# Gate tiles, a reciprocal and the first mixed input, reordered in a kernel of two transformer blocks

## What is computed

```python
# first block, in each of two layers, behind the mixers
x = x + concat(mixers) @ w_out[l]
u = rms_norm(x, mlp_norm_g[l]) @ w_up[l]
x = x + square(relu(u)) @ w_down[l]
gate = sigmoid(rms_norm(x, ple_norm_g[l]) @ w_ple_gate[l])
e = rms_norm(p[l] @ w_ple_proj[l], ple_post_norm_g[l])
x = x + gate * e                       # followed by rms_norm(x) @ next weights

# second block, second layer (RWKV-7), h = rms_norm(x, norm_tok)
xx = 0.5 * (h[t - 1] + h[t + 1]) - h   # neighbours in time, zero outside
xr = h + xx * mu[0]                    # and xw, xk, xv, xa, xg with mu[1..5]
r = xr @ w_r                           # and so on for w, k, v, a, g
```

## Time and profile before

| what | before |
|---|---|
| median of 3 runs | 3337.2 us (3335.54 to 3346.71) |
| the profiled execution | 3335.55 us, of which the profile's span is 3333.5 us |
| PE busy | 3062.7 us (92%) |
| PE weight loads busy | 2431.1 us (73%) |
| VectorE / ScalarE / GpSimd busy | 1870.9 / 1384.1 / 633.8 us |
| mean granted clock of TensorE | 0.966 of 2.4 GHz |

### The profile page before, as it was taken

How to read it: one execution, slowest core, us unless ns; L and a number is a source line. 1 busy time by engine, 2 the same in 40 slices (tenths; PEclk the granted TensorE clock), 3 DMA queues, 4 the chain that set the end, 5 groups by cost and what they waited for, 6 DMA issues and landing times. The chain is left out here.

```text
span 3333.5 us, 57339 instructions
## 1 busy us (share of the span) xinstructions
PE 3062.7 (92%) x24238; PEld 2431.1 (73%) x24238; DVE 1870.9 (56%) x2687; ACT 1384.1 (42%) x2354; POOL 633.8 (19%) x528
## 2 busy tenths in 40 slices
PE   8979999999978999999989999979788988799999
PEld 6756788887745788886757888757477777588887
DVE  6675543435675452536575746564366776457464
ACT  5545322235445421224274423335465565344232
POOL 1000220212000230302000101133164564101010
PEclk9989999999989999999899999979899999899999
DMA  4101222222101222222003322225411111033232
GB/s 154 46 1 61 86 96 97 94 92 82 64 4 45 82 95 95 95 97 76 20 1 120 100 97 95 89 101 180 152 47 38 38 45 41 18 111 103 89 101 81
DMA packets 82333, 260.91 MB, mean 78 GB/s; under 512 B 9632, under 2 KB 13216, under 8 KB 81696
## 3 DMA queue, kind: packets, MB, share of 16 engines
q1 hardware_dynamic: 71424, 235.75, 21.7%
q10 hardware_dynamic: 10656, 21.50, 1.7%
HBM read 236.25 MB, written 20.97 MB: 77 GB/s over the span
## 5 line engine op out<-in xcount | busy, mean ns | idle before, releaser
L1645 DVE TENSOR_TENSOR mlp_w_lo<-mlp_ring,mlp_w_hi 128x1024 fp32r<-128x1024 f32 (+1 forms) x211 | 251.3, 1192 | 598.3 <-ACT mlp_w_hi L1625 598.1
L1625 ACT ACTIVATE mlp_w_hi<-mlp_ring 128x1024 fp32r<-128x1024 f32 (+1 forms) x211 | 213.2, 1011 | 695.9 <-PE ps L1586 689.3
L1645 DVE TENSOR_TENSOR ffn_w_lo<-ffn_ring,ffn_w_hi 128x1024 fp32r<-128x1024 f32 (+3 forms) x172 | 222.5, 1294 | 446.9 <-ACT ffn_w_hi L1625 446.9
L1625 ACT ACTIVATE ffn_w_hi<-ffn_ring 128x1024 fp32r<-128x1024 f32 (+3 forms) x172 | 187.3, 1089 | 486.3 <-PE ps L1586 480.7
L1585 PE MATMUL ps<-mlp_more_parts,mlp_w_hi 128*128 128x512 f32 x952 | 374.6, 394 | 0.0
L1584 PE MATMUL ps<-tiles_parts,mlp_w_hi 128*128 128x512 f32 x832 | 331.0, 398 | 5.7 <-issue 5.7
L1584 PE MATMUL ps<-ffn_x_parts,ffn_w_hi 128*128 128x512 f32 x792 | 312.1, 394 | 22.7 <-DVE ffn_x_parts L2355 20.9
L1584 PE MATMUL ps<-mlp_more_parts,mlp_w_hi 128*128 128x512 f32 x760 | 307.9, 405 | 25.6 <-DVE mlp_more_parts L1698 15.0
L1586 PE MATMUL ps<-tiles_parts,mlp_w_lo 128*128 128x512 f32 x832 | 329.0, 395 | 0.0
L1585 PE MATMUL ps<-ffn_x_parts,ffn_w_hi 128*128 128x512 f32 x792 | 309.8, 391 | 0.0
L1586 PE MATMUL ps<-ffn_x_parts,ffn_w_lo 128*128 128x512 f32 x792 | 309.7, 391 | 0.0
(11 more groups left out here) (494 smaller groups left out, 6233.3 us busy)
## 6 DMA issues: line engine op xcount, KB each, us to landing
ffn_ring<-in_w_ffn_up SPq DMA_DIRECT2D x88, 512.0 KB, 3.3
mlp_ring<-in_w_up SPq DMA_DIRECT2D x64, 512.0 KB, 3.4
mlp_ring<-in_w_down SPq DMA_DIRECT2D x64, 512.0 KB, 3.4
rwkv_keep<-ffn_ring ACTq DMA_DIRECT2D x64, 256.0 KB, 2.4
sq<-rwkv_keep SPq DMA_DIRECT2D x64, 256.0 KB, 3.0
ffn_ring<-in_w_ffn_down SPq DMA_DIRECT2D x16, 768.0 KB, 4.3
in_ring<-in_w_in SPq DMA_DIRECT2D x22, 512.0 KB, 3.4
mlp_ring<-in_w_in SPq DMA_DIRECT2D x22, 512.0 KB, 3.3
```

The costliest lines, as they stand in the source:

```text
L1625: nc.scalar.activation(w.w_hi[:, n % SPLIT, 0:width], w.ring[:, n % RING, 0:width], ACT.Copy).then_inc(s["w_hi_ready"], 1)
L1645: nc.vector.tensor_tensor(w.w_lo[:, n % SPLIT, 0:width], w.ring[:, n % RING, 0:width], w.w_hi[:, n % SPLIT, 0:width].bitcast(F32), ALU.sub ...
```

## The change

Five edits:

- `chain` gets a flag, `urgent`. The steps of a product's last tile may then come ahead of that iteration's rounding and split of weights, on ScalarE and VectorE.
- The gate sets it. Within a step the sigmoid is of tile t itself, x's addition and the next input's high half, square and low half are of tile t - 1, the squares' sum of tile t - 2, and one step follows the last tile and not four.
- The MLP norm's reciprocal moves from step 5 to step 7 of the embedding's product.
- r's input is no longer made from the difference. VectorE prepares mu/2 and 1 - mu once; ScalarE scales h by 1 - mu (`kept_h`, two places); VectorE adds mu/2 times the neighbours' sum. The eight differences, which the other inputs need, are made in a row behind r's low halves. r's first two tiles run in step.
- The store of x for the RWKV layer's end is issued behind the root and not ahead of it, and a square root of one column is put ahead of the last tile's square, which loads the activation table there.

```diff
@@ class Linear (and Small): a flag urgent, False by default @@
@@ chain @@
+    def divided(n):
+
+        todo = list(steps(n))
+        first = 1 if todo and todo[0][0].urgent and todo[0][1] == todo[0][0].tiles - 1 else 0
+        return todo[:first], todo[first:]
...
             for n in range(len(slots) + SPLIT):
+                ahead, behind_split = divided(n - SPLIT)
+                for lin, t in ahead:
+                    lin.on_act(act, s, lin, t)
                 if n < len(slots):
                     rounded(n)
-                for lin, t in steps(n - SPLIT):
+                for lin, t in behind_split:
                     if lin.on_act:
                         lin.on_act(act, s, lin, t)
...
@@ PostNorm.linear @@
         def on_dve(dve, s, lin, t):
-            if t == 5:
+            if t == DT - 1:
                 self.normed.invert(dve, s)
@@ gated_embedding @@
-        if 2 <= t < 2 + DT:
-            dve.wait_ge(s["gated"], t - 1)
-            nc.vector.tensor_tensor(m.x[:, t - 2, :], m.x[:, t - 2, :], sq[:, 4 + (t - 2) % 4, :], ALU.add).then_inc(s["gate_added"], 1)
-        if t >= 4:
-            then.dve(dve, s, t - 4)
+        if t >= 1:
+            dve.wait_ge(s["gated"], t)
+            nc.vector.tensor_tensor(m.x[:, t - 1, :], m.x[:, t - 1, :], sq[:, 4 + (t - 1) % 4, :], ALU.add).then_inc(s["gate_added"], 1)
+            then.dve(dve, s, t - 1)
...
-        if 1 <= t <= DT:
-            lin.wait_free(act, s, t - 1)
-            nc.scalar.activation(sq[:, (t - 1) % 4, :], sq[:, (t - 1) % 4, :], ACT.Sigmoid).then_inc(s["gate_ready"], 1)
-        if 3 <= t < 3 + DT:
-            then.act(act, s, t - 3)
+        if t < DT:
+            lin.wait_free(act, s, t)
+            nc.scalar.activation(sq[:, t % 4, :], sq[:, t % 4, :], ACT.Sigmoid).then_inc(s["gate_ready"], 1)
+        if t >= 1:
+            then.act(act, s, t - 1)
...
-        if 3 <= t < 3 + DT:
-            then.pool(pool, s, t - 3)
+        if t >= 2:
+            then.pool(pool, s, t - 2)
...
-    return Linear(a["w_gate"], layer * DT, DT, DT, normed.rhs, normed.arrived, 1, {0: normed.sums}, on_act, on_dve, on_pool, last=4)
+    return Linear(a["w_gate"], layer * DT, DT, DT, normed.rhs, normed.arrived, 1, {0: normed.sums}, on_act, on_dve, on_pool, last=1, urgent=True)
@@ WkvInputs.product: in_step=which == "r" @@
@@ WkvInputs.follow @@
+        mu = self.vec[:, VR["mu"]:VR["mu"] + DT]
+        halved, kept = self.first_mu[:, 0, :], self.first_mu[:, 1, :]
         def on_act(act, s, lin, t):
             if t < DT:
+                if t == DT - 1:
+                    nc.scalar.activation(self.table[:], m.eps[:, 0:1], ACT.Sqrt)
                 lin.wait_free(act, s, t)
                 tok.square(act, s, t)
                 return
+            tok.root(act, s)
             nc.scalar.dma_start(self.x_kept, m.x[:]).then_inc(s["x_saved"], 16)
-            tok.root(act, s)
+            act.wait_ge(s["mu_ready"], 2)
             for j in range(DT + 2):
                 if j < DT:
                     act.wait_ge(s["h_ready"], j + 1)
+                    if j >= 2:
+                        act.wait_ge(s["mixed"], j - 1)
+                    nc.scalar.activation(self.kept_h[:, j % 2, :], m.h[:, j, :], ACT.Copy, scale=kept[:, j:j + 1]).then_inc(s["kept_ready"], 1)
                     nc.scalar.activation(m.sq[:, j, 0:S:S - 1], m.h[:, j, 1:S - 1:S - 3], ACT.Copy).then_inc(s["edges_ready"], 1)
                 if j >= 2:
                     self.mix_hi(act, s, "r", j - 2)
...
+                if t == 0:
+                    nc.vector.tensor_scalar(halved, mu, 0.5, None, ALU.mult).then_inc(s["mu_ready"], 1)
+                    nc.vector.tensor_scalar(kept, mu, -1.0, 1.0, ALU.mult, ALU.add).then_inc(s["mu_ready"], 1)
                 return
             tok.invert(dve, s)
-            for j in range(DT + 3):
+            dve.wait_ge(s["mu_ready"], 2)
+            for j in range(DT + 2):
                 if j < DT:
                     nc.vector.scalar_tensor_tensor(out=m.h[:, j, :], in0=m.x[:, j, :], scalar=self.gain[:, j:j + 1], in1=m.rstd[:],
                                                    op0=ALU.mult, op1=ALU.mult).then_inc(s["h_ready"], 1)
                 if 1 <= j <= DT:
+                    k = j - 1
                     dve.wait_ge(s["near_ready"], j)
                     dve.wait_ge(s["edges_ready"], j)
-                    nc.vector.scalar_tensor_tensor(out=m.sq[:, j - 1, :], in0=m.sq[:, j - 1, :], scalar=0.5, in1=m.h[:, j - 1, :],
-                                                   op0=ALU.mult, op1=ALU.subtract).then_inc(s["xx_ready"], 1)
-                if 2 <= j <= DT + 1:
-                    self.mix(dve, s, "r", j - 2)
-                if j >= 3:
-                    dve.wait_ge(s["mix_hi"], j - 2)
-                    self.rest(nc.vector, "r", j - 3).then_inc(s["mix_lo"], 1)
+                    dve.wait_ge(s["kept_ready"], j)
+                    if k >= 4:
+                        dve.wait_ge(s["mix_lo"], k - 3)
+                    nc.vector.scalar_tensor_tensor(out=self.acc[:, k % 4, :], in0=m.sq[:, k, :], scalar=halved[:, k:k + 1], in1=self.kept_h[:, k % 2, :],
+                                                   op0=ALU.mult, op1=ALU.add).then_inc(s["mixed"], 1)
+                if j >= 2:
+                    dve.wait_ge(s["mix_hi"], j - 1)
+                    self.rest(nc.vector, "r", j - 2).then_inc(s["mix_lo"], 1)
+            for j in range(DT):
+                dve.wait_ge(s["mixed"], j + 1)
+                nc.vector.scalar_tensor_tensor(out=m.sq[:, j, :], in0=m.sq[:, j, :], scalar=0.5, in1=m.h[:, j, :],
+                                               op0=ALU.mult, op1=ALU.subtract).then_inc(s["xx_ready"], 1)
```

More of the change, by code:

```diff
@@ L1476, with __init__ @@
 class Linear:
-    def __init__(self, weights, base, tiles, ks, rhs, arrived, parts=1, after_first=None, on_act=None, on_dve=None, on_pool=None, last=0, in_step=False):
+    def __init__(self, weights, base, tiles, ks, rhs, arrived, parts=1, after_first=None, on_act=None, on_dve=None, on_pool=None, last=0, in_step=False, urgent=False):
         self.weights, self.base, self.tiles, self.ks, self.parts = weights, base, tiles, ks, parts
         self.rhs, self.arrived, self.after_first = rhs, arrived, after_first
-        self.in_step = in_step
+        self.in_step, self.urgent = in_step, urgent
         self.on_act, self.on_dve, self.on_pool, self.last = on_act, on_dve, on_pool, last
@@ L1501, in __init__ @@
     def __init__(self, emit, on_act):
-        self.emit, self.on_act, self.on_dve, self.on_pool = emit, on_act, None, None
+        self.emit, self.on_act, self.on_dve, self.on_pool, self.urgent = emit, on_act, None, None, False
         self.place, self.banks = [], BANKS
@@ L1650, in _ @@
             for n in range(len(slots) + SPLIT):
+                ahead, behind_split = divided(n - SPLIT)
+                for lin, t in ahead:
+                    lin.on_dve(dve, s, lin, t)
                 if n < len(slots):
                     rest(n)
-                for lin, t in steps(n - SPLIT):
+                for lin, t in behind_split:
                     if lin.on_dve:
@@ L2252, in __init__ @@
         self.wide = own.enter_context(nc.sbuf_tensor("wkv_wide", [P, D], F32))
-        self.low_g = w.square
+        self.first_mu = own.enter_context(nc.sbuf_tensor("wkv_first_mu", [P, 2, DT], F32))
+        self.table = own.enter_context(nc.sbuf_tensor("wkv_table", [P, 1], F32))
+        self.low_g = self.kept_h = w.square
         self.out = w.ring[:, :, DT * P:DT * P + S]
         self.tok = Normed(nc, m, w, "tok", gain, None, None)
-        self.signals = ["tok_squared", "tok_added", "tok_summed", "tok_root", "tok_rstd", "h_ready", "near_ready", "edges_ready", "xx_ready",
+        self.signals = ["tok_squared", "tok_added", "tok_summed", "tok_root", "tok_rstd", "mu_ready", "h_ready", "kept_ready", "near_ready", "edges_ready", "xx_ready",
                         "mixed", "mix_hi", "mix_lo", "low_ready", "low_hi", "low_lo", "wide_in", "x_saved",
@@ L2331, in on_pool @@
                 self.mix_lo(pool, s, i, k)
-        return Linear(weights, 0, tiles, DT, lambda k: (home[k], home[DT + k]), arrived, 1, None, on_act, on_dve, on_pool, last=1 if which == "g" else 0)
+        return Linear(weights, 0, tiles, DT, lambda k: (home[k], home[DT + k]), arrived, 1, None, on_act, on_dve, on_pool, last=1 if which == "g" else 0,
+                      in_step=which == "r")
     def low_rest(self, dve, s, t):
```

## The result

| | before | after |
|---|---|---|
| median | 3337.2 us (5 runs) | 3314.7 us (5 runs, 3311.4 to 3316.8) |
| ratio, 95% interval | | 0.9929 [0.9916, 0.9943] |
| the profiled execution, its span | 3335.55, 3333.5 us | 3314.73, 3312.9 us |
| mean granted clock | 0.966 | 0.969 |

The kernel is 22.5 us (0.7%) faster by the medians; 21.45 had been forecast, 3315.75 against 3314.7.

A forecast was written before the change was run, and what follows sets the result against it. PE, busy for all but some 8% of the span, was taken as the bound. Savings of 10.4 + 8.3 + 2.75 = 21.45 us off the 3337.2 us median gave 3315.75 us, range 3307 to 3326.

The forecast's parts named there:

- The likeliest case: The forecast itself: 21.45 us saved over three places, median 3315.75 us, chance 0.57.
- A: Gate's end, each layer: next tile 7.0 us earlier, less 1.8 for slow clock; 5.2 a layer, 10.4 in all.
- B: MLP norm's reciprocal, each layer: PE starts 2.35 us earlier, clock returns 1.8; 4.15 a layer, 8.3 in all.
- C: r's inputs, once: third tile's products 4.15 us earlier, 1.4 given back later; 2.75 us.
- T: End of the last gate tile, about 774.4 us in the profile before; k7, the next product's last input, forecast 9.05 later.
- The slow stretch behind it: Half clock on PE after the gate-end pause of 4.2 us, taken to cost 1.8 us a layer.
- Rival (1): Clock eats it: gate-end pause costs 3.1 us, MLP-start slow stretch stays; 15.45 us saved, 3321.8 us; chance 0.18.
- the eight rounds: Split-and-mix rounds r3 to r7, w, k0, k1: 5.63 us each against PE's 5.45, giving back 1.4 us.
- Small pieces: Table load, x's store and two short multiplications, moved or added in pauses of ScalarE and VectorE: worth nothing.
- Rival (2): No pause worth the name at the gate's end, no slow stretch; 29.9 us saved, 3307.3 us; chance 0.12.
- (3): Almost nothing gained: the split behind the gate's last steps becomes the wait; 9.7 us saved, 3327.5 us; chance 0.10.
- (4): Slower: VectorE's round in each gate tile passes 8.5 us, so PE waits at each of 14 tiles; chance 0.03.

The follow-up runs named there:

- no_ahead: Changed kernel with the gate's urgent flag off, so the last gate steps come behind the weights' split again; ratio to the kernel before 0.9932.
- both: Changed kernel with both last gate steps ahead of the weights' split and VectorE's two mixes ahead of its copy; 3302.2 us, ratio to the kernel before 0.9898.
- no_table: Changed kernel without the one-column square root, so the activation table loads behind the last square again; one execution, no ratio given.
- a_only: Kernel before with only the flag and the gate's edit; median 3329.1 us, ratio to the kernel before 0.9967.
- before_again: Kernel before, unchanged, profiled once more as a control; one execution, no ratio given.
- two_ahead: Changed kernel with both last gate steps, not only the first of the two, ahead of the weights' rounding and split; ratio to the kernel before 0.9916.

## Why the prediction was right

**The mechanism and the sum.** The likeliest case held at each place, and each term lies within its bounds. By the local measures the terms are: A 4.86 + 5.25 = 10.1 us (forecast 10.4), B 2 x 3.77 = 7.5 (8.3), C 3.5 (2.75); together 21.1, against 21.45. That the sum is off by so little is in part luck: B is 0.8 too large and C 0.75 too small. The two profiled executions are 20.8 apart, the medians 22.5; what is left is within the spread of runs, and so is the nearness of 3315.75 to 3314.7.

**A** came as worked out. The one pause is 4.20 us (4.2), k7 at T + 8.96 (9.05), one turn lost to GpSimd's additions. The slow stretch behind it, priced at 1.8 us: in the window of 12 us from 780 the granted clock is 0.81, 2.3 us of it lost; in the second layer (1541 to 1553) 0.86, so 1.7. Rival (1) priced it at 3.1, by a reading that was wrong: in the old tail the granted clock is 1.00 again at 791.5 and not at 793.1 (a window of 791.0 to 792.5 has 0.84, one of 792.5 to 795 has 1.00; the row of 0.80 at 792.51 is one product behind the sums), so 4.6 us at half clock behind 786.91, 2.3 us. That is what the first layer of after lost. The second half of rival (1), a slow stretch left at B, is gone too. One choice of the text was of no use: the turn ahead of the split carries none of the gain (no_ahead), and the prediction, which put the product of tile 7 "now ahead of the split", had not asked what the other order would give. So the depth was right as the cause of A, and the flag was no part of it.

**B**. PE starts 2.30 us earlier against the embedding's split before it (forecast 2.35), by (370.30 - 364.32) - (368.24 - 364.56), and the clock came back. The two rows of VectorE that this counts from, before and after:

```profile
364.32 1.35 DVE L1645 TENSOR_TENSOR mlp_w_lo<-mlp_ring,mlp_w_hi 128x256 fp32r<-128x256 f32 x1 [1.99 <-ACT mlp_w_hi L1625]
...
364.56 1.35 DVE L1654 TENSOR_TENSOR mlp_w_lo<-mlp_ring,mlp_w_hi 128x256 fp32r<-128x256 f32 x1 [2.00 <-ACT mlp_w_hi L1631]
```

What the clock returned is 3.77 - 2.30 = 1.47 us; the term said 1.8. That term was sized too large by 0.33 a layer.

**C** was worth more than forecast, 3.5 against 2.75, and two of its statements were off. First product: 3.25 us earlier (3.1), pitch 2.77 (2.9), last low half 4.5 earlier (3.6). The mis-sized term is the pitch, and it was a sum added up wrong: the durations that the text lists (0.05 + 0.63 + 0.2 + 0.63 + 0.6 + 0.66) make 2.77, as measured, and not 2.9. Five tiles have that pitch, 5 x 0.13 = 0.65 us; the first product and the last two low halves give 0.15 each. So r2's first product came 5.05 earlier, not 4.15, and less the 1.4 of the eight rounds that is 3.6, as the distances have it (3.5). And "the step order wins nothing" was wrong: it is worth 0.8 to 1.0 us. As forecast, the third tile's split stands behind the eight differences (0.6 each: 4.89), and PE waits 2.12 us there (about 2). As forecast too, each later round shows as 5.64 us (5.63) where PE would take 5.45. That these rounds are set by the order of the queues and not by VectorE's load is what `both` shows: with the same work they take 5.04.

**Small pieces.** The table load moved for 0.09 us, as good as nothing. The store and the two short multiplications were not tried by themselves; C0 is 3.37 in no_table, which has them, and 3.38 in a_only and before_again, which don't.

**Slips without weight.** A's path adds up to T + 8.96 by its own terms (7.5 + 0.72 + 0.74), as measured, where the text has 9.05; B's pause was to be 2.86 - 2.35 = 0.5 us and not 0.7 (0.58 measured); the upper bounds of A and B, 7.1 and 4.5 a layer, are stated without a working (A's terms give 6.9).

**Rival (2)**, no pause at A, is what two_ahead and both come near: 2.13 us of pause. **(3)** and **(4)** have nothing for them: no round of a gate tile makes PE wait, and A's wait is one in each layer.

## What to carry to other kernels

Where PE is nearly always busy, look for waits followed by a slow stretch: a pause of 3 to 4 us cost another 1.5 to 2.3 us. When a tail is shortened, ask of each step on the path whether it still queues behind a weights' split; one step ahead brought nothing here, two brought 3 us a layer. Eight independent operations that are queued in a row belong where PE has work in hand, and which of two operations of an engine comes first (copy or mix) can set the pitch of a stage: here 5.64 us, or 5.04 until PE itself set the pace. Below 0.3% of a span, measure distances inside one execution, with an unchanged kernel as a control.
